# Groups behind a norm in three units tile by tile, a new first group, and a few transfers moved

## The reference, cut to what matters

```
x = x + 0.5 * swiglu(rmsnorm(x, ffn1_norm), ffn1_w_gu, ffn1_w_down)
h = rmsnorm(x, mix_norm);  z = h @ w_in          # spatial gating, latent attention, memory attention
x = x + merged @ w_out
x = x + 0.5 * swiglu(rmsnorm(x, ffn2_norm), ffn2_w_gu, ffn2_w_down)
sh1, sc1, g1, sh2, sc2, g2 = split(silu(c) @ ada_w + ada_b, 6)      # "conditioning"
hl = rmsnorm(x, norm1_g) * (1 + sc1) + sh1
x = x + g1 * short_conv_mixer(hl)
x = x + g2 * swiglu_2(rmsnorm(x, norm2_g) * (1 + sc2) + sh2)
return rmsnorm(x, final_g)
```

## Time and profile before

| | us |
|---|---|
| median of the runs | 917.33 |
| profiled execution | 917.23 |
| its span, first to last instruction | 915.48 |
| TensorE busy | 897.0 |
| VectorE busy | 619.1 |
| ScalarE busy | 458.4 |

### The profile page before, as it was taken

The page is one execution under the profiler, slowest core; times in us unless marked ns, Lnnn a source line. Parts: engine busy times, 40 slices in busy tenths (PEclk is TensorE's granted clock), DMA queues, the critical chain, the costliest instruction groups (busy, mean ns, idle before and its releaser), DMA issues.

```text
span 915.5 us, 11297 instructions
## 1 busy us (share of the span) xinstructions
PE 897.0 (98%) x4228; PEld 748.2 (82%) x4228; DVE 619.1 (68%) x870; ACT 458.4 (50%) x684; POOL 43.2 (5%) x62
## 2 busy tenths in 40 slices
PE   6999999999999999999999999999999999999997
PEld 5888888888988888888788888887888788888885
DVE  4887977548458867686768777647767845555653
ACT  6464545435579376446545444443444344444540
POOL 1010000013103000000000000001000100000001
PEclk9999999999999999999999999999999999999999
DMA  9787777555545455454697777754655465555541
GB/s 340 283 307 263 281 278 274 212 198 196 176 155 184 161 191 168 153 179 143 213 359 281 258 281 279 277 185 146 253 186 176 164 226 187 188 188 187 181 149 47
DMA packets 55855, 195.74 MB, mean 214 GB/s; under 512 B 6856, under 2 KB 7288, under 8 KB 55800
## 3 DMA queue, kind: packets, MB, share of 16 engines
q1 hardware_dynamic: 55800, 195.01, 60.1%
HBM read 193.91 MB, written 1.07 MB: 213 GB/s over the span
## 4 chain that ended last, share of the span: by engine, by line
PE 95%; DVE 2%; issue 1%; DMA 1%; POOL 0%; ACT 0%; SPq 0%; POOLq 0%; DVEq 0%; ACTq 0%
PE ps L637 29%; PE ps L639 29%; PE ps L638 29%; PE ps L673 2%; PE ps L582 1%; PE ps L589 1%; DMA t_X<-in_x 1%; PE ps L772 1%; PE ps L788 1%; DVE t_wl L1100 1%; POOL t_sc L1542 0%; PE ps L730 0%; PE ps L764 0%; PE ps L712 0%; PE ps L779 0%
## 5 line engine op out<-in xcount | busy, mean ns | idle before, releaser
L1100 DVE TENSOR_TENSOR t_wl<-t_raw,t_wh 128x1024 fp32r<-128x1024 f32 (+2 forms) x308 | 364.2, 1209 | 130.1 <-ACT t_wh L829 127.7
L829 ACT ACTIVATE t_wh<-t_raw 128x1024 fp32r<-128x1024 f32 (+2 forms) x308 | 311.3, 1045 | 141.9 <-DMA t_raw<-in_f_up 83.9
L637 PE MATMUL ps<-t_wh,t_XH 128*128 128x512 f32 (+2 forms) x656 | 257.4, 392 | 0.8 <-DVE t_wl L1100 0.8
L639 PE MATMUL ps<-t_wh,t_XL 128*128 128x512 f32 (+2 forms) x656 | 253.6, 387 | 0.0
L638 PE MATMUL ps<-t_wl,t_XH 128*128 128x512 f32 (+2 forms) x656 | 253.4, 386 | 0.0
L639 PEld LDWEIGHTS ps<-t_wh,t_XL 128*128 128x128 f32 x656 | 123.4, 188 | 24.9
L637 PEld LDWEIGHTS ps<-t_wh,t_XH 128*128 128x128 f32 x656 | 123.5, 188 | 24.6 <-DVE t_wl L1100 1.3
L638 PEld LDWEIGHTS ps<-t_wl,t_XH 128*128 128x128 f32 x656 | 123.6, 188 | 23.3
L637 PE MATMUL ps<-t_wh,t_YH 128*128 128x512 f32 x288 | 113.4, 394 | 0.0
L639 PE MATMUL ps<-t_wh,t_YL 128*128 128x512 f32 x288 | 112.2, 390 | 0.0
L638 PE MATMUL ps<-t_wl,t_YH 128*128 128x512 f32 x288 | 112.1, 389 | 0.0
(11 more groups left out here) (214 smaller groups left out, 606.8 us busy)
## 6 DMA issues: line engine op xcount, KB each, us to landing
t_raw<-in_f_up SPq DMA_DIRECT2D x132, 512.0 KB, 4.0
t_raw<-in_f_dn SPq DMA_DIRECT2D x66, 512.0 KB, 3.2
t_raw<-in_ada SPq DMA_DIRECT2D x48, 512.0 KB, 4.5
t_raw<-in_mkv SPq DMA_DIRECT2D x8, 512.0 KB, 3.2
t_raw<-in_ga SPq DMA_DIRECT2D x8, 512.0 KB, 3.5
t_raw<-in_gc SPq DMA_DIRECT2D x8, 512.0 KB, 3.4
t_raw<-in_gb SPq DMA_DIRECT2D x8, 512.0 KB, 3.4
t_raw<-in_wo SPq DMA_DIRECT2D x8, 512.0 KB, 3.5
```

Source lines behind the costliest of these rows:

```text
L637: pe.matmul(o, xh, h, start=k == 0, stop=False)
L639: x = pe.matmul(o, xl, h, start=False, stop=k == n - 1)
L829: act.activation(wh[:, m % SPL, 0:w], raw[:, n % RAW, 0:w], ACT.Copy).then_inc(hi_made, 1)
L1100: dve.tensor_tensor(wl[:, n % RAW, 0:w], raw[:, n % RAW, 0:w], wh[:, m % SPL, 0:w].bitcast(F32), ALU.subtract).then_inc(drained, 1)
```

## The change

- `wide` groups behind a norm have three units instead of four; the fourth is a normal unit behind them.
- In a tail, a split is fed in front of the second matmul unit of tile 0, and those that stood among tile 1's units go (the first product's tail keeps them).
- `head`: in f2_up0 tile 1's turn stands in front of the third unit; in the other two it stands behind the three units of tile 0.
- The first group gets a list of its own (`first`): dummy transposes on TensorE (`warm`, 16 and 14), x turned in four blocks (tile, half) and split straight from PSUM with the gain applied, four units tile by tile.
- x comes by two DMAs of 512 KB that ScalarE issues; SyncE begins with the first weights.
- ScalarE's first table load is called by a small copy at the start. The conditioning's vector is made six units later, its 48 steps and the load of `mem` stand later in the stream.
- At the end VectorE scales 640 columns and ScalarE 384; each part is one DMA, ScalarE's issued by itself.

```diff
-            while ada and i >= 4 and (24 - len(ada)) * 50 < (i - 3) * 24:
+            while ada and i >= 10 and (24 - len(ada)) * 50 < (i - 9) * 24:
...
+    def first():
+        S.extend([("warm", 0), ("split", 0), ("xturn", 0, 0), ("split", 1), ("xturn", 0, 1), ("warm", 1), ("split", 2), ("split", 3)])
+        at["stream"] = at["split"] = 4
+        before = {(0, 2): [("xturn", 1, 0)], (0, 3): [("xturn", 1, 1), "feed"], (1, 0): ["feed"],
+                  (1, 1): ["feed"], (1, 2): ["feed"], (1, 3): [("stats",)]}
...    (for t, for m: the steps of before, then ("mm", "f1_up0", m, t))
     def ups(f, extra, head):
...
-                if g == 0 and head:
+                if g == 0 and f == "f1":
                     if i == 0:
-                        wide([(f"{f}_up0", m) for m in range(4)], head)
+                        first()
+                    continue
+                if g == 0 and head and i < 3:
+                    if i == 0:
+                        wide([(f"{f}_up0", m) for m in range(3)], head)
...
     def tail(p):
-        steps = {(1, 0): [("half", p, 1, 0), ("rms", p, 0)], (1, 1): [], (1, 2): ["feed"], (1, 3): ["feed"]}
+        steps = {(0, 1): ["feed"], (1, 0): [("half", p, 1, 0), ("rms", p, 0)], (1, 1): [], (1, 2): [], (1, 3): []}
         if p == "wo":
...
-            steps[1, 2] = [("xturn2", 0, 1), "feed"]
+            steps[1, 2] = [("xturn2", 0, 1)]
         if p in ("f2", "co"):
...
-            steps[1, 3] = [("nturn", p, 0, 0), ("nturn", p, 0, 1), "feed"]
+            steps[1, 3] = [("nturn", p, 0, 0), ("nturn", p, 0, 1)]
+        if p == "f1":
+            steps[1, 2] = steps[1, 3] = ["feed"]
...
     def head(p):
         if p == "wo":
-            return {(0, 1): [("xturn2", 1, 1)]}
-        return {(0, 3): [("nturn", p, 1, 0), ("nturn", p, 1, 1)]}
+            return {(0, 2): [("xturn2", 1, 1)]}
+        return {(1, 0): [("nturn", p, 1, 0), ("nturn", p, 1, 1)]}
...
-    extra = {0: [("stats",)], 1: [("cond", 0)], 3: [("load_mem",)], 8: [("load_rows",)], ...
+    extra = {6: [("cond", 0)], 7: [("load_mem",)], 8: [("load_rows",)], ...
...
-            wide([("conv_cc0", m) for m in range(4)], head("f2"))
-            S.append(("load_mod", 1))
+            wide([("conv_cc0", m) for m in range(3)], head("f2"))
+            unit("conv_cc0", 3, ("load_mod", 1))
...    (TensorE)
+                if name == "f1_up0" and i in (0, 2):
+                    pe.wait_ge(*x_lo.at(t, i // 2))
+            def warm(n):
+                for _ in range((16, 14)[n]):
+                    pe.transpose(ps[:, 3, 0:P], ident[:, :], ident[:, :])
...    (ScalarE)
+            def consts_():
+                for t in (0, 1):
+                    act.dma_start(X[:, t, :], A["x"][t]).then_inc(x_in[t], 16)
+                act.wait_ge(*consts.at("mhalf"))
+                act.activation(col("first"), mhalf[:, 0:1], ACT.Copy)
+            def xturn(t, j):
...    (four ACTIVATE of 128 x 128, PSUM to XH, scale = the gain's column)
-                o = acc2[:, t, 512:1024]
+                o = acc2[:, t, 640:1024]
                 act.activation(o, o, ACT.Copy, scale=col("r", "f3", t)).then_inc(final1, 1)
+                act.wait_ge(final1, t + 1)
+                act.dma_start(out[t][:, 640:1024], o).then_inc(stored, 16)
...    (VectorE, xturn: four scalar_tensor_tensor of 128 x 128, PSUM * gain - XH to XL)
...    (SyncE)
             def consts_():
-                sp.dma_start(cols[:, 0:A["cols"].shape[1]], A["cols"]).then_inc(cols_in, 16)
-                for j in (0, 1):
-                    for t in (0, 1):
-                        sp.dma_start(X[:, t, half_of(j)], A["x"][t][:, half_of(j)]).then_inc(x_in[t][j], 16)
-                    if j == 0:
-                        fetch(0)
-                for n in range(1, RAW):
+                for n in range(RAW):
                     fetch(n)
+                    if n == 0:
+                        sp.dma_start(cols[:, 0:A["cols"].shape[1]], A["cols"]).then_inc(cols_in, 16)
```

More of the change, by code:

```diff
@@ L152, in wide @@
             tick()
+    def first():
[4 more added lines that the diff above has]
+        for t in (0, 1):
+            for m in range(4):
+                for step in before.get((t, m), []):
+                    if step == "feed":
+                        feed_to(at["split"] + 1)
+                    else:
+                        S.append(step)
+                S.append(("mm", "f1_up0", m, t))
     def ups(f, extra, head):
@@ L219, in head @@
         if p == "wo":
-            return {(0, 1): [("xturn2", 1, 1)]}
-        return {(0, 3): [("nturn", p, 1, 0), ("nturn", p, 1, 1)]}
+            return {(0, 2): [("xturn2", 1, 1)]}
+        return {(1, 0): [("nturn", p, 1, 0), ("nturn", p, 1, 1)]}
     S.extend([("consts",), ("load_cond", 0)])
[L224 to L228, removed]
+    extra = {6: [("cond", 0)], 7: [("load_mem",)], 8: [("load_rows",)], 12: [("mem_sq", 0)], 13: [("mem_sq", 1)],
              15: [("mem_row", 0), ("mem_row", 1)], 17: [("mem_turn", 0), ("mem_turn", 1)],
@@ L453, in build @@
         landed = [sem(f"raw{i}") for i in range(RAW)]
-        x_in = [[sem(f"x{t}{j}") for j in (0, 1)] for t in (0, 1)]
+        x_in = [sem(f"x{t}") for t in (0, 1)]
         mem_in, cols_in, rows_in, mid_in, bgate_in, final_in, stored, cond_in, mod_out, mrow_in, grow_in = (
@@ L478, in build @@
         scaled = Signal(sem("scaled"), steps("scaled"))
+        x_hi, x_lo = Signal(sem("x_hi"), steps("xturn")), Signal(sem("x_lo"), steps("xturn"))
         norms = [k for k in steps("nturn") if k[0] != "f1"]
@@ L610, in mm @@
                     pe.wait_ge(*out_of(GROUPS[q - 2][0], t))
-                if name in ("f1_up0", "mkv0") and t == 0:
-                    pe.wait_ge(parted, ring["x" if name == "f1_up0" else "mem", i] + 1)
+                if name == "f1_up0" and i in (0, 2):
+                    pe.wait_ge(*x_lo.at(t, i // 2))
+                if name == "mkv0" and t == 0:
+                    pe.wait_ge(parted, ring["mem", i] + 1)
                 if name in ("conv_cc0", "f3_up0") and i in (0, 2):
@@ L646, in consts_ @@
                 pe.wait_ge(*consts.at("ident"))
-            def xturn(j):
-                b = through_tmp(("x", j))
-                for t in (0, 1):
-                    if j % 2 == 0:
-                        pe.wait_ge(x_in[t][j // 2], 16)
-                    pair(b, X, t, 2 * j, t == 0)
+            def warm(n):
+                for _ in range((16, 14)[n]):
+                    pe.transpose(ps[:, 3, 0:P], ident[:, :], ident[:, :])
+            def xturn(t, j):
+                b = bank(("x", t, j), *x_lo.at(t, j))
+                if j == 0:
+                    pe.wait_ge(x_in[t], 16)
+                quad(b, X, t, j)
             def mem_turn(j):
@@ L809, in gate_turn @@
                     pair(b, GB, t, 2 * j, t == 0)
-            part = {"mm": mm, "consts": consts_, "xturn": xturn, "mem_turn": mem_turn, "ada_rows": ada_rows,
+            part = {"mm": mm, "consts": consts_, "warm": warm, "xturn": xturn, "mem_turn": mem_turn, "ada_rows": ada_rows,
                     "hid_turn": hid_turn, "nturn": nturn, "xturn2": xturn2, "lat_turn": lat_turn,
@@ L844, in cond_, with xturn @@
                 act.activation(cond, cond, ACT.Silu).then_inc(cond_made, 1)
-            def xturn(j):
-                if j == 0:
-                    act.wait_ge(cols_in, 16)
-                into_tmp(("x", j), 2, 256, C["ffn1"][:, 2 * j:2 * j + 2])
+            def consts_():
+                for t in (0, 1):
+                    act.dma_start(X[:, t, :], A["x"][t]).then_inc(x_in[t], 16)
+                act.wait_ge(*consts.at("mhalf"))
+                act.activation(col("first"), mhalf[:, 0:1], ACT.Copy)
+            def xturn(t, j):
+                b, full = place["x", t, j]
+                if (t, j) == (0, 0):
+                    act.wait_ge(cols_in, 16)
+                act.wait_ge(turned, full)
+                for c in range(4):
+                    k = 4 * j + c
+                    m = act.activation(XH[:, k, t * P:t * P + P], ps[:, b, c * P:c * P + P], ACT.Copy,
+                                       scale=C["ffn1"][:, k:k + 1])
+                m.then_inc(*x_hi.by(t, j))
             def stats():
                 for t in (0, 1):
-                    act.wait_ge(x_in[t][0], 16)
-                    act.wait_ge(x_in[t][1], 16)
+                    act.wait_ge(x_in[t], 16)
                     act.activation((FG[:, :], acc2[:, 1, :])[t], X[:, t, :], ACT.Square, scale=1 / 32,
@@ L1078, in final @@
                 act.wait_ge(*with_gain.at(t, 1))
-                o = acc2[:, t, 512:1024]
+                o = acc2[:, t, 640:1024]
                 act.activation(o, o, ACT.Copy, scale=col("r", "f3", t)).then_inc(final1, 1)
-            part = {"split": split, "cond": cond_, "xturn": xturn, "stats": stats, "mem_sq": mem_sq_,
+                act.wait_ge(final1, t + 1)
+                act.dma_start(out[t][:, 640:1024], o).then_inc(stored, 16)
```

(22 more changed lines are left out.)

## The result

The kernel after takes 922.15 us (median; 921.12 to 923.58), the one before 916.97 in the same session: a ratio of 1.0056 (95% interval 1.0043 to 1.0069). The sign and both new waits came as predicted; two terms of the sum did not, in opposite directions.

What follows compares the result with a forecast made beforehand. TensorE, 95% of the chain, was taken as the bound, so only its waits or slow stretches count. Terms -0.3 - 0.5 + 2.1 + 2.1 - 0.1 = +3.3, with the clock +4.1, gave 921.3 us; range 917.6 to 923.6.

Steps and rivals of the forecast that it cites:

- The sign: Whole kernel: slower than before, chance 0.78, against 0.13 for no change and 0.09 for faster.
- both new waits: Behind f2 and co: TensorE idle 2.5 to 3.5 us before the third unit, then 1 us before tile 1's first unit.
- f2 to conv_cc0: Boundary behind f2: +2.1 us (+0.7 to +2.6), waits of 3.8 instead of 1.75, the third unit's split behind tile 1's rows.
- co to f3_up0: Boundary behind co: +2.1 us by the same list, with a wait of 3.35 before the third unit.
- The clock: Pauses behind f2 and co: TensorE's clock falls to half; one fall charged at 0.8 us (0 to 2.3 for both).
- Rival B: Clock falls in both pauses at full price, or the start lands late (+1.5): 922.8 us, chance 0.22.
- The start: Beginning to the end of the first group: -0.3 us (-2.8 to +1.2), first matmul near 10.5 us.
- R: Time when both the first weights and tile 0 of x have landed: taken as 7.0 us, break-even 7.3, upper end 8.5.
- Rival C: A much faster start, landing at 5.0 us (-2.3), and no fall of the clock: 918.5 us, chance 0.10.
- wo to f2: Boundary behind wo: -0.5 us (-1.4 to +0.2), a wait of 0.8 in place of 1.4.
- The end: Last steps and store: -0.1 us (-0.4 to +0.2), since the stores' bytes flow without a break.
- what was put at nothing: Conditioning steps and their weights, the conditioning's silu, the load of mem and the f1 tail's extra split: cost 0.

Runs made afterwards that it cites:

- e3: The changed kernel plus 22 and 28 dummy transposes in front of the third unit behind f2 and co: 919.63 us, ratio 1.0024 to the kernel before.
- e2: The changed kernel with one more split fed during tile 0 of wo, f2 and co, before tile 1's rows: 912.90 us, ratio 0.9951.
- g3: Against g2, SyncE issues the gains and both tiles of x first and the weights behind them: 914.83 us, ratio 0.9964 to the kernel before.
- g2: Against e4, SyncE issues x between and behind the first weights and the gains, ScalarE nothing: 912.67 us, ratio 0.9948 to the kernel before.
- e4: Against e2, four units wide again, with tile 1's turn in front of tile 0's fourth unit: 911.62 us, ratio 0.9937 to the kernel before.
- g1: Against e4, no dummy transposes at the start: 913.17 us, ratio 0.9952 to the kernel before.

## Why the prediction was right, and where its sum was not

**f2 to conv_cc0 and co to f3_up0: right.** Waits of 2.7 and 3.35 were forecast, 2.6 and 3.35 came, each with 1.1 for the low part behind it (1.07). Without the clock's share the two steps are 2.22 and 2.25 (e3) against 2.1. What carried it was to read VectorE's list in order and ask who waits at its end; e2 shows that the split's place in that list is the cause.

**The clock: the term that was mis-sized.** "I charge one fall with 0.8 (0 to 2.3 for both places)" was 2.8 to 2.9 (1.5 + 1.3 by e3's steps; 2.9 by the ratios). It fell at both places, and each fall cost more than 0.8. The step that failed is "part of the slow time here passes while TensorE waits anyway". In the first pause none did: the low clock is granted as TensorE starts again, so six matmuls at 0.2 each (1.2) and the eight transposes (0.3) pay for it in full. In the second some 0.4 of it passed in the wait (727.8 to 728.17), and the price was 1.3. The rows shown did not say when in a pause the fall comes: in the earlier trace rows no work followed.

Nor do they make a rule of the 2.4 us without work after which the clock fell there. The last matmul of after ends at 913.85, and TensorE does nothing from then on; the clock still stands at 1.00 in this stretch and falls at 918.84, 5.0 us behind that matmul:

```profile
916.50:918.00 1.50, 0.00 (x0) 0.00 (x0) 0.76 (x2) 0.62 (x1) 0.63 (x1) 1.00 0.00 0
```

In the traces of the eight experiments the same distance is 2.7 to 5.2. So a pause of 2.6 or 3.35 may also pass without a fall; that the clock would fall in both did not follow from "longer than that". Rival B had both falls, with 1.5 more and so 2.3 in all, some 0.5 too little; that its 922.8 is near the 922.53 of the profiled execution is luck, since the start came 1.0 earlier than it had it.

**The start: mis-sized the other way.** "R = 7.0, nearer the upper row" was 5.5, and the first matmul came at 9.27, not near 10.5. The bytes (1.12 MB) had moved by some 5.1, and the landing came 0.4 behind them, not 2.3 as in the trace of before: there the first weights stood behind cols and half of x in one queue. With x and cols in front again (g3) the first weights land at 8.35 again, and in one queue with the weights first (g2) R is 5.9; so what weighed in R is weights first. What the 0.5 for fuller slices and the 0.9 for issues and smaller packets are worth each, no run shows. In time, the order of g3 costs 0.7 to 1.0, and 2.2 with the fall in the wait that it makes; the one queue of g2 costs 1.05, most of it by the second weights. The first step behind R was nearly right, R + 3.5 = 9.0 against 9.27; the end was 0.5 short, R + 15.9 = 21.4 against 21.9 in the measure of the chain. 0.4 of that is VectorE's wait for the second weights, which the sum did not have. So R gave -1.5, and the start -1.0 against the forecast. Rival C had the early landing (R = 5.0), but no fall with it.

**wo to f2: right**, -0.55 against -0.5, by the mechanism forecast. The timeline there, against the earlier trace rows:

```profile
436.63 0.69 DVE L1275 TENSOR_TENSOR t_X<-ps,t_X 128x512 f32<-128x512 f32 x1 [0.45 <-PE ps L658]
...
439.06 1.23 DVE L1137 TENSOR_TENSOR t_wl<-t_raw,t_wh 128x1024 fp32r<-128x1024 f32 x1 [1.74 <-ACT t_wh L852]
...
440.34 0.50 PE L656 MATMUL ps<-t_wh,t_YH 128*128 128x512 f32 x1 [0.59 <-DVE t_wl L1137]
```

The rows come early, VectorE then idles 1.74, and the split behind them costs TensorE 0.8, as forecast: from the turn's start at 439.15 to the next matmul lie 1.19, in e4, with that split in front, 0.36 (439.09 to 439.45). (The bracket's 0.59 counts from the modelled end of the turn.) e4 gains 1.45 here.

**The end, and what was put at nothing.** +0.09 against -0.1, inside its bounds. The conditioning steps cost nothing, as said; the 0.23 gained at f2 was not foreseen.

The two wrong sizes, some +2.0 for the clock and -1.0 for the start, partly cancel, which is luck. The range held the result although the clock's 2.8 lay outside the term's own bounds (0 to 2.3); the 0.85 between forecast and median is no measure of how well the terms were known.

## What to carry to other kernels

On an engine that works through a list in order, a step that another engine needs early goes ahead of a chain of dependent steps, not behind it: here one split's place behind tile 1's rows is worth 922.15 against 912.90. Where TensorE must pause as here (2.6 and 3.35 us), count the wait and the clock apart, and charge the low clock to the work that comes after the pause, as a price that may or may not fall due; useless transposes in the pause (e3) took that part away, and an order without the pause (e2, e4) took both. At the start, order the first transfers by who waits for them (here weights, then x): x first cost 0.7 to 1.0, and 2.2 where the clock fell in the wait; one queue instead of two cost 1.05.

## What the hardware showed that was not expected

The view prints a clock of 1.00 for the first microseconds, where no record of the clock exists. In after, sixteen transposes take 0.23 each at the start and fourteen 0.13 each later (start us, us), with 1.00 printed for both; the first record in that trace begins at 7.48. In before it begins at 13.28 and in g1 at 13.42, where in both the matmuls go from 0.43 apart to 0.23. Ahead of the first record only the pitch tells:

```profile
1.61 3.68 PE L670 MATMUL ps<-t_ident 128*128 128x128 f32 x16 [1.61 <-POOL t_sc L1596]
...
7.29 1.79 PE L670 MATMUL ps<-t_ident 128*128 128x128 f32 x14
```

A transfer's time from issue to landing depends strongly on what stands in front of it in its queue: the same 512 KB of first weights took 3.9 us in front (g2) and 6.2 behind cols and x (g3).
